# A table in DRAM beside a hybrid attention and PEER kernel: zero blocks written during the weight loads, and 256 indirect scatters per layer

## The reference, cut to what matters

```
x = layer_norm(alpha*x + mix(x))     # MLA and sparse attention, gated, then w_out
x = layer_norm(alpha*x + peer(x))

def peer(x):                         # 8 heads, 128 x 128 experts of one neuron each
    s = scores of the query halves against 2 x 128 sub-keys per head
    top 16 of each half -> 256 sums -> the best 16 (expert i*128+j), softmax -> gate
    a = expert_u[experts] . x ;  w = gate * gelu(a) ;  y = sum of w * expert_v[experts]
```

## Time and profile before

| what | value |
|---|---|
| runs | 2196.02 and 2198.08 us, median 2197.05 |
| profiled execution, first to last instruction | 2194.3 us (2.75 us under the median of the runs) |
| PE busy | 2136.5 us (97%) |
| DVE, ACT, POOL busy | 1500.2 (68%), 1156.8 (53%), 181.5 us (8%) |
| granted TensorE clock, mean | 0.996 |
| DMA | 350.24 MB, mean 160 GB/s; 1.05 MB of it written to DRAM |

### The profile page before, as it was taken

How to read it: one execution, slowest core, us unless ns; L and a number is a source line. 1 busy time by engine, 2 the same in 40 slices (tenths; PEclk the granted TensorE clock), 3 DMA queues, 4 the chain that set the end, 5 groups by cost and what they waited for, 6 DMA issues and landing times.

```text
span 2194.3 us, 41496 instructions
## 1 busy us (share of the span) xinstructions
PE 2136.5 (97%) x14244; PEld 1917.2 (87%) x14244; DVE 1500.2 (68%) x2796; ACT 1156.8 (53%) x1835; POOL 181.5 (8%) x202
## 2 busy tenths in 40 slices
PE   8999999999999999999999999999999999999997
PEld 6987899999997788888788888999999977888886
DVE  6666767777778855555676566777777797555556
ACT  4456445544458755445444464444544596444443
POOL 1100000000007400000020000000000182000000
PEclk9999999999999999999999999999999999999999
DMA  5622455555550256666565234555555503665664
GB/s 187 198 86 88 155 165 182 182 183 183 182 180 27 59 191 193 201 203 198 160 197 167 88 106 154 166 183 183 183 183 182 166 0 101 195 201 191 200 204 134
DMA packets 97584, 350.24 MB, mean 160 GB/s; under 512 B 11312, under 2 KB 11344, under 8 KB 97520
## 3 DMA queue, kind: packets, MB, share of 16 engines
q1 hardware_dynamic: 94320, 338.69, 48.3%
q0 software_dynamic: 3200, 10.66, 1.6%
HBM read 348.26 MB, written 1.05 MB: 159 GB/s over the span
## 4 chain that ended last, share of the span: by engine, by line
PE 85%; DMA 4%; DVE 4%; ACT 2%; issue 2%; POOL 1%; POOLq 0%; DVEq 0%; SPq 0%; ACTq 0%
PE wide L1536 33%; PE acc L1521 13%; PE acc L1522 13%; PE acc L1523 13%; PE acc L2003 4%; DMA raw<-in_front 2%; DMA raw<-in_peer_v 2%; PE tr L1714 1%; POOL hot_i L574 1%; ACT hot_i L844 1%; PE acc L1874 1%; ACT hi L601 1%; PE acc L1876 1%; PE acc L1875 1%; PE wide L1972 1%
## 5 line engine op out<-in xcount | busy, mean ns | idle before, releaser
L601 ACT ACTIVATE hi<-raw 128x1024 fp32r<-128x1024 f32 (+1 forms) x644 | 676.3, 1051 | 540.7 <-DMA raw<-in_peer_v 341.9
L919 DVE TENSOR_TENSOR lo<-raw,hi 128x1024 fp32r<-128x1024 f32 x520 | 636.8, 1225 | 448.6 <-ACT hi L601 445.6
L1521 PE MATMUL acc<-xT_hi,lo 128*128 128x256 f32 x2544 | 724.9, 285 | 5.9 <-DVE kr L1132 3.2
L1522 PE MATMUL acc<-xT_lo,hi 128*128 128x256 f32 x2544 | 721.1, 283 | 0.0
L1523 PE MATMUL acc<-xT_hi,hi 128*128 128x256 f32 x2544 | 721.0, 283 | 0.0
L1521 PEld LDWEIGHTS acc<-xT_hi,lo 128*128 128x128 f32 x2544 | 489.4, 192 | 12.6 <-issue 4.6
L1522 PEld LDWEIGHTS acc<-xT_lo,hi 128*128 128x128 f32 x2544 | 489.6, 192 | 0.0
L1523 PEld LDWEIGHTS acc<-xT_hi,hi 128*128 128x128 f32 x2544 | 489.5, 192 | 0.0
L1536 PE MATMUL wide<-hi,w_lo 128*128 128x512 f32 x1016 | 313.9, 390 | 5.4 <-DVE w_lo L1462 5.2
L1536 PE MATMUL wide<-lo,w_hi 128*128 128x512 f32 x1016 | 312.9, 389 | 0.0
L1536 PE MATMUL wide<-hi,w_hi 128*128 128x512 f32 x1016 | 312.8, 389 | 0.0
(11 more groups left out here) (307 smaller groups left out, 1943.2 us busy)
## 6 DMA issues: line engine op xcount, KB each, us to landing
raw<-in_peer_u SPq DMA_DIRECT2D x256, 512.0 KB, 3.5
raw<-in_peer_v SPq DMA_DIRECT2D x254, 512.0 KB, 3.5
raw<-in_front SPq DMA_DIRECT2D x114, 512.0 KB, 3.5
ln_par<-in_ln POOLq DMA_DIRECT2D x10, 512.0 KB, 5.6
raw<-in_front SPq DMA_DIRECT2D x12, 384.0 KB, 3.2
w<-in_cmp_w POOLq DMA_DIRECT2D x16, 256.0 KB, 4.3
raw<-in_front SPq DMA_DIRECT2D x8, 312.0 KB, 3.4
xs<-in_x SPq DMA_DIRECT2D x2, 512.0 KB, 4.6
```

The costliest lines, as they stand in the source:

```text
L601: nc.scalar.activation(hi[:, s, :width], raw[:, s, :width], ACT.Identity).then_inc(hi_done, 1)
L919: nc.vector.tensor_tensor(lo[:, s], raw[:, s], hi[:, s].bitcast(F32), ALU.subtract).then_inc(lo_done, 1)
L1521: mm(dst, lo[:, s, c], xh[:, k], start=k == 0, stop=False)
L1522: mm(dst, hi[:, s, c], xl[:, k], start=False, stop=False)
```

## The change

Each layer gets a table in DRAM of 128 x 128 x 256 float32 (16.8 MB), which nothing reads.

- **Zero blocks.** A zeroed SBUF tile `blank` (128 x 256) is written into the table in 64 parts per layer (`blank_part`), each 256 KB in runs of 1 KB. SP issues them: one behind each of the front's first 44 tile loads (in layer 1 the first four follow behind the first four loads), and the other 20 in a row behind the 44th, ahead of the load of tile 44. SP waits once, before all of this, for `blanked`.
- **Scatters.** Behind LayerNorm 1's inverse square roots GpSimd waits for the 64 parts, then issues 256 indirect transfers per layer. Each writes one float32 from each of the 128 partitions of `iota` to a place in the table read from a column of `spots`; in layer 0 it adds to what is there, in layer 1 it replaces it. After every 16 GpSimd waits until all of them have landed.
- `spots` is filled once by an `iota` at the start, `blank` by a `memset` ahead of the first parameter load.

```diff
+        blank = small("blank", [P, SEQ])
+        spots = small("spots", [P, TOPK], U32)
+        table = [nc.dram_tensor(f"table{l}", (NKEYS * P * SEQ, 1), F32, kind="Internal").ap() for l in range(DEPTH)]
...
+            def blank_part(l, c):
+
+                part = table[l].rearrange("(j i t) o -> i j (t o)", j=NKEYS, i=P)[:, bass.ds(c * 2, 2)]
+                sp.dma_start(part, blank[:].unsqueeze(1).broadcast_to([P, 2, SEQ])).then_inc(table_blank, 16)
...
                         sp.dma_start(raw[:, s], src[l, q * SLOTS + (skip + s)]).then_inc(loaded[s], 16)
+                        if blanks:
+                            blank_part(l, q * SLOTS + (skip + s))
...
+            sp.wait_ge(blanked, 1)
             for l in range(DEPTH):
                 if l == 0:
-                    load(l, t["front"], 0, T_UQ // SLOTS)
+                    load(l, t["front"], 0, T_UQ // SLOTS, 0, True)
                 else:
                     load_past_own(l, T_A)
-                    load(l, t["front"], SLOTS, T_UQ // SLOTS - 1, SLOTS)
+                    for c in range(SLOTS):
+                        blank_part(l, c)
+                    load(l, t["front"], SLOTS, T_UQ // SLOTS - 1, SLOTS, True)
                 for n in range(T_UQ, T_UKV):
                     load_part(l, n, width_of(n))
-                load(l, t["front"], T_UKV, (T_BR - T_UKV) // SLOTS, T_UKV)
+                    blank_part(l, n)
+                load(l, t["front"], T_UKV, (T_BR - T_UKV) // SLOTS, T_UKV, True)
+                for c in range(T_BR, NKEYS // 2):
+                    blank_part(l, c)
...
+            nc.gpsimd.memset(blank[:], 0.0).then_inc(blanked, 1)
             ln_load(0)
...
+            pst.link(nc.gpsimd.iota(spots[:], [[SEQ, TOPK]], 0, NKEYS * SEQ + 1, allow_small_or_imprecise_dtypes=True))
...
                 for tt in range(TT):
                     rsqrt(5 * l + R_LN1 + tt, tt, tt + 1)
+
+                pool.wait_ge(table_blank, (l + 1) * NKEYS // 2 * 16)
+                for i in range(TT * HEADS):
+                    for k in range(TOPK):
+                        pool.indirect_dma_start(table[l], bass.IndirectOffsetOnAxis(spots[:, k:k + 1], 0), iota[:, k:k + 1], None,
+                                                compute_op=ALU.add if l == 0 else ALU.bypass).then_inc(table_added, 16)
+                    pool.wait_ge(table_added, (l * TT * HEADS + i + 1) * TOPK * 16)
 
                 pool.wait_ge(tr_read[X_PK % 2], OPEN + l * (NTR // 2) + NTR // 2)
```

More of the change, by code:

```diff
@@ L421, in build @@
         stored = sem("stored")
+        blanked = sem("blanked")
+        table_blank = sem("table_blank")
+        table_added = sem("table_added")
         apart = sem("apart")
@@ L434, in _, with load @@
             sp.dma_start(freq[:], t["freq"].partition_broadcast(P)).then_inc(pos_loaded, 16)
-            def load(l, src, first, turns, skip=0):
+            def blank_part(l, c):
+                part = table[l].rearrange("(j i t) o -> i j (t o)", j=NKEYS, i=P)[:, bass.ds(c * 2, 2)]
+                sp.dma_start(part, blank[:].unsqueeze(1).broadcast_to([P, 2, SEQ])).then_inc(table_blank, 16)
+            def load(l, src, first, turns, skip=0, blanks=False):
                 with sp.Fori(0, turns) as q:
@@ L503, in _ @@
         def _(pool):
-            pst = Steps(pool, pool_step, 0, 10)
+            pst = Steps(pool, pool_step, 0, 11)
             def ln_load(i):
```

## The result

The changed kernel took **2402.0 us** (median of 2 runs, 2396.25 and 2407.75) against 2197.05 before: ratio 1.0933, interval 1.0911 to 1.0955. The forecast was 2207 with a range of 2197 to 2400; the time lies 2 us above its upper end. The profiled run took 2396.25 with a span of 2394.1, 199.8 more than the span before.

What follows compares the result with a forecast made beforehand. TensorE, busy 97% of the span, was taken as the bound, with scatters hidden in GpSimd's idle time. Start 0.3 + 1, chain 4 and burst 5 make 10 us; 2194.3 + 2.75 + 10 = 2207 us, range 2197 to 2400.

Steps and rivals of the forecast that it cites:

- The scatters, issue: GpSimd's issue of each indirect transfer: 1.09 us taken, 0.53 + 0.56, between bounds of 0.53 and 2.05.
- rival B: Up-projection: VectorE's two-SBUF-input instructions slow scatters to 1.56 us on average; GpSimd 24 us late, 2255 us; chance 0.24.
- C: The scatters' issue alone is heavy, 2.05 us each, and layer 0 also adds: 150 us late per layer, 2507; chance 0.12.
- The budget of 398.9 us: GpSimd's room per layer for scatters, from its last square root at 260.92 to the latest return for `first_i` at 659.80.
- a return d us later costs about d: After the up-projection: ScalarE's in-order wait for `first_i` stands before the last U tile's copy, so GpSimd's lateness costs equally.
- Landings: GpSimd's wait after every 16 scatters: 1.5 us each, 24 us per layer.
- Rival D: Small writes fill the DMA engines in the up-projection at 0.18 us per element: 200 us more per layer, 2600; chance 0.09.
- Their load on the DMA engines: Up-projection: 2048 scattered elements per engine and layer fit in 165 us free, up to 0.08 us per element.
- I take 0.8 us: DMA time of one 256 KB zero block, between bounds of 0.62 and 2.9 us.
- the burst's length: Front: 21 zero blocks queued behind tile 43 take 16.8 us, delaying tile 44 to 187.4; 5 us lost in two layers.
- Ahead of tile 44 there are five such loads: 4 us: Front: in both layers together, five tile loads on the chain of waits are each lengthened 0.8 us by a block.
- it fits, with longer latencies: Front: a tile and a block need 2.3 us of DMA time at full rate within a tile's 2.88 us.

Runs made afterwards that it cites:

- the three variants: Changed kernel, both layers replacing, with 512-byte rows, 64 partitions per scatter, or two awaited fills before each scatter: 2257.33, 2238.08 and 2466.75 us on the third chip.
- half width: Changed kernel with both layers replacing and each scatter writing from 64 partitions instead of 128: 2238.08 us on the third chip, 2888.13 on the fourth.

## Why the prediction was wrong

**The step that failed is "The scatters, issue".** It took 1.09 us, a direct issue plus one small GpSimd instruction, and the bounds were 0.53 and 2.05. Start to start it is made of these parts:

| us per scatter | taken | layer 0, adds | layer 1, replaces |
|---|---|---|---|
| undisturbed | 1.09 | 1.56 | 0.96 |
| gap to the next instruction | 0 | 0.30 | 0.30 |
| held up by VectorE | 0 (0.47 in rival B) | about 0.19 | about 0.20 |
| landing waits, spread | 0.09 | 0.14 | 0.16 |
| sum | 1.18 | 2.19 | 1.62 |

The line on VectorE is what the start-to-start times of 2.19 and 1.62 us leave; the others are read. Three things were missing together. The 0.30 us between two issues in a row were never put down; the change has 256 of them per layer, 77 us, and no row of the trace before could show them, since it has no long sequence of issues on GpSimd. The price of the addition, 0.60 us, was named under C and not carried into the sum, though the diff says that only layer 0 adds. And "describing 128 rows is the same work" as a direct issue was an argument by likeness. That its 1.09 us came near the 0.96 of a replacing scatter was luck, since no row showed one of either kind.

**The frame held.** The budget of 398.9 us, "a return d us later costs about d", and "`first_i` is late next" are what the trace shows: 162.7 us late at ScalarE, 161.4 lost. Half of the scatters cost nothing beyond the blocks (2220.65 for 2220.01). With 2.19 and 1.62 us (landings included) in place of 1.18, the prediction's own working gives 256 x 2.19 - 398.9 = 162 and 256 x 1.62 - 398.9 = 16 us late, 2207 + 162 + 16 = 2385 us; the 13 us that the blocks cost beyond their 10 make 2398.

**Landings.** 24 us per layer were taken; 35.5 and 41.8 came, 2.4 and 2.8 us per wait for 1.5. Small beside the issue.

**Rival B** had the right mechanism and too high a price. It took 49% of 0.96 us, 0.47; the runs show 0.19 to 0.28 us on average, since a scatter is held only if it starts inside the instruction, and for what is left of it. Two inputs in SBUF are not needed for it: the one-input form held scatters too. The Trainium skill, page "SBUF — State Buffer", section "Who interferes with whom", puts down, as an inference, that descriptor generation needs the write side. By its rule on two-input instructions the trace agrees (1.69 us beside L947, 0.96 without); by its rule on descriptor generation, from which nothing would be lost beside L947, it does not, for an indirect transfer, and the measurement decides.

**Rival C**, a heavy issue, comes nearest in layer 0: 2.19 us for its 2.05. It stood at 0.12 and was priced for both layers, where it holds for one.

**Rival D** falls. In layer 1 the DMA share is 0.55 with the scatters and 0.58 before. In layer 0 it is 0.69, so an added element takes (0.69 - 0.56) x 2.19 x 16 / 128 = 0.04 us of an engine (0.56 is the share with the blocks alone), half of the 0.08 that would be too much. "Their load on the DMA engines: it fits" was right. A read-modify-write below 512 bytes, as the Trainium skill has it on the page "DMA: Bandwidth & Descriptors", section "Specifications", leaves no trace in the DMA share of the replacing layer.

**The blocks** cost 23.5 us for 10. "I take 0.8 us" was right (0.76), and so was the burst's length (15.9 us for 16.8). Two other terms were small. "Ahead of tile 44 there are five such loads: 4 us" took those already on the chain; in the window from 45 to 60 us the engines moved 286 GB/s at a share of 0.88 for 223 at 0.71, and TensorE was busy for 13.14 of 15 us where it had been for all. The sentence "it fits, with longer latencies" was half right: the latencies put new loads on the chain, which has six in layer 0 ahead of the burst where it had one. And tile 44 landed 5.56 us after issue, not 3.5, from a start 5.9 us later: at 195.04 for 187.4.

**The chances.** 0.44 stood on slower by over 2%, 0.55 on the same; the sum's own range up to 2245 was far too narrow for a price that no row showed.

## What to carry to other kernels

Price a row of like instructions by start to start, with the gap between them, and multiply both by the count: 0.30 us was nothing once and 77 us in a layer. Where 256 of a new kind hang on one price taken by likeness, and the break-even (1.46) lies between its bounds (0.53 and 2.05), that is the forecast: near even chances, not a likeliest case. And run a control on the same chip as the variant: on the third chip three theories looked confirmed; on the fourth one of them fell (half the writes) and one held only in part (512 bytes).

## What the runs showed of the hardware

An indirect scatter of one element per partition holds GpSimd for 0.96 us if it replaces and 1.56 us if it adds, with 128 partitions (0.90 and 1.41 with 64), and the next follows 0.30 us later. 128 elements in place of one do not change it (median 962 ns). To the DMA engines an adding scatter from 128 partitions is 144 packets, a replacing one 32.

A scatter that starts while VectorE makes `lo` ends 0.83 us (replacing) or 1.42 us (adding) after that instruction; with less than 0.15 us of it left it is not lengthened. The adding ones show the same 1.42 us with two inputs (TENSOR_TENSOR, 1.22 us) and with one (TENSOR_SCALAR, 0.73 us).

Replacing scatters 1.3 to 1.6 us apart can hold up TensorE's instructions, and only these, from one matmul per 0.12 us to one per 2.1 to 2.8 us, until 15 us after the last. On three chips it was seen in every layer that replaced at this pace, in part only where rows of 512 bytes were written; it was not seen on the chip where the three variants ran alone, nor in the first measurement of the changed kernel. It was never seen with adding scatters (2.03 us apart or more) or with replacing ones 2.04 us apart. The waits between groups, the spacing of the addresses, the number of partitions and the rate of packets are ruled out as its cause; longer rows weaken it. Open stays what in the chip is shared by the two, whether it is the operation or the pace that spares the adding scatters, and why the same kernel stalls on one chip and not on another (2888 and 2238 us at half width).
